# Two expert stages of a hybrid model on one Trainium2 core: a down unit and half a gate unit placed half a slot further back

## The chip, the cores and the metric

The kernel runs on one core of one Trainium2 chip. The metric is the device time in microseconds (us). Every weight comes from device memory (HBM) while the kernel runs, and the same core computes both layers. TensorE, the matmul engine, is called PE in the profile, its weight load PEld; VectorE is DVE, ScalarE is ACT, GpSimd is POOL, and SyncE, which issues nearly all loads, is SP. A DMA instruction issued on SP joins one queue and is served by the core's 16 DMA engines in order of issue. 1 MiB below is 1,048,576 bytes, and a full "unit" of weights is 4 MiB.

## The reference, cut to what matters

Two layers (a recurrent mix, then a gated linear attention) are each followed by a mixture of 32 experts over 272 tokens (256 and 16 meta tokens), all in 32-bit floats. Each token uses 2 experts of one group, but all experts' weights are needed: 3 MiB each, 96 MiB a layer.

```python
def hier_moe(h, w_group, b_group, w_router, b_router, w_gate, w_up, w_down):
    ...
    combine = jnp.sum(jax.nn.one_hot(expert_idx, N_EXPERTS, dtype=jnp.float32) * weights[..., None], axis=1).astype(h.dtype)
    y = jnp.zeros_like(hf)
    for e in range(N_EXPERTS):
        hid = jax.nn.silu(hf @ w_gate[e]) * (hf @ w_up[e])
        y = y + (hid @ w_down[e]) * combine[:, e:e + 1]
    return y.reshape(B, T, D)
```

## The kernel before, in words

An expert stage (`y` = 0 for the first layer, 1 for the second) takes the experts in 8 groups of 4 (`q` = 0 to 7). Tokens are gathered per expert into a tile of at most 32 rows, so that 4 experts fill 128 partitions. Each group has three units of weights: gate, up and down. So a stage has 24 units, `u = 3 * q + kind`, each 4 experts x 2048 floats in each partition (4 MiB). For gate and up the 2048 floats are 8 blocks of 256 over the contraction index k; for down they are 2 blocks of 1024.

There are four slots in the on-chip memory (`slots[0]` to `slots[3]`, each as large as one unit), and `UNIT_SLOT[y][u]` says which slot a unit uses. For units 0 to 11 they simply go round. In the first stage these are slots 1, 2, 3, 0 and again; in the second 0, 1, 2, 3. `UNIT_PREV[y][u]` is the unit that was in the slot before. A slot's lower half of every expert is its columns `0:D` (D = 1024), the upper half `D:2 * D`.

**The load side** is one program on SP, `experts(y)`. It goes through the units in order and issues most units as two DMAs of 2 MiB, each with rows of 8 KiB (line 449). Ahead of each it waits until the unit that was last in the slot is done (line 419, semaphore `unit_done`, which PE raises by one at the end of each unit). A few units at the start of a stage are cut up. Unit 4 (up, q = 1) has its first half laid aside in other buffers (`aside`), and its second half goes to the lower half of its slot as soon as the first half of gate 0 has been used (`half_done`). Unit 5 (down, q = 1) goes half by half: its lower half on `half_done`, its upper half on the unit before it in the slot, unit 1 (lines 421 to 427 for y = 0, lines 444 to 447 for y = 1). In the first stage one expert's quarter of unit 5 (`down[:, 7, 0:D]`) is issued early, at line 406, since a quarter of unit 1 lies elsewhere and leaves that place free. Unit 6 (gate, q = 2) and all that follow wait for a whole slot. After unit 11 SP waits for unit 8, and may load experts for overflowing tokens (lines 452 to 467) into the slot of unit 8; in the first stage of this run that happens once.

**The compute side** is one program on PE. For every group it runs, in this order, the gate unit (line 1531, 64 matmuls), the sums of the group before into the output (`combine`, lines 1491 and 1493), the up unit (line 1531), transposes and gathers (lines 1484, 1590, 1476), and the down unit (line 1603, 32 matmuls of 512 columns). `loaded(u)` makes PE wait for the load. The last down unit of a stage (unit 23) comes in four DMAs of 1 MiB (line 433); two of them (`ld_last0`) must be there for the first call of line 1671. After the first stage the weights of the second layer's projection come in (lines 484 and 488).

Of the kernel before, what the change touches and what calls it, by code (L numbers as in the profile page):

```python
# [14 lines left out]
D = 1024  # L15
KD = D // P
# [15 lines left out]
NU = 3 * NQ  # L32
# [25 lines left out]
UNIT_SLOT = [[1, 2, 3, 0] * 3 + [2, 3, 0, 1, 2, 3, 0, 1, 2, 0, 1, 3], [0, 1, 2, 3] * 3 + [1, 2, 3, 0, 1, 2, 0, 3, 1, 0, 2, 3]]  # L58
UNIT_PREV = [[max([v for v in range(u) if x[v] == x[u]], default=None) for u in range(NU)] for x in UNIT_SLOT]
UNIT_TURN = [[sum(x[v] == x[u] for v in range(u)) for u in range(NU)] for x in UNIT_SLOT]  # L60
FIRST_LAYER = [UNIT_SLOT[0][:NU - 1].count(j) for j in range(4)]
OV_SLOT = [1, 0]
OV_UNIT = 8
OV_NEXT = 15
# [24 lines left out]
def program(nc, a, out, y_dram):  # L89
    ctx = ExitStack()  # L90
    with ctx:
# [61 lines left out]
        def s(name):  # L153
            if name not in S:
                S[name] = sem(name)
            return S[name]
# [135 lines left out]
        def _(sp):  # L292
# [49 lines left out]
            def experts(y):  # L342
# [23 lines left out]
                for u in range(NU):  # L366
# [13 lines left out]
                    if u == 0:  # L380
                        if y == 0:
                            sp.wait_ge(s("oc_set"), NC)
                        else:
                            sp.wait_ge(s("mix_part"), 1)
                    elif u == 1 and y == 1:
                        sp.wait_ge(s("mix_part"), 4)
                    elif u == 3:
                        sp.wait_ge(s("res_done"), (4, 9)[y])
                        sp.dma_start(slots[j][:, 0:2, :], gate[:, 4:6, :]).then_inc(s(f"ld_s{j}"), 16)
                        if y == 0:  # L390
                            sp.wait_ge(s("res_done"), 5)
                            sp.dma_start(slots[j][:, 2, :], gate[:, 6, :]).then_inc(s("ld_wout"), 16)
                            sp.wait_ge(s("res_done"), 6)
                            sp.dma_start(yst[0], up[:, 3, 0:D]).then_inc(s("ld_pv_ys"), 16)
                            sp.dma_start(slots[j][:, 3, :], gate[:, 7, :]).then_inc(s(f"ld_s{j}"), 16)
                            continue
                        sp.wait_ge(s("res_done"), 11)
                    elif u == OV_NEXT:
                        if y == 0:
                            sp.wait_ge(s("ov_free"), passes)  # L400
                        else:
                            sp.wait_ge(s("ov_fin"), y + 1)
                    elif u == 4:
                        set_aside(2 + y)
                        if y == 0:
                            sp.dma_start(slots[UNIT_SLOT[y][5]][:, 3, 0:D], down[:, 7, 0:D]).then_inc(s("ld_lruw_e5"), 16)
                        if y == 0:
                            sp.wait_ge(s("half_done"), 1)
                            sp.dma_start(slots[j][:, 3, 0:D], up[:, 7, 0:D]).then_inc(s("ld_half"), 16)
                            sp.dma_start(slots[j][:, 0:3, 0:D], up[:, 4:7, D:2 * D]).then_inc(s(f"ld_s{j}"), 16)  # L410
                            sp.wait_ge(s("unit_done"), UNIT_PREV[y][u] + 1)
                            sp.dma_start(slots[j][:, 3, D:2 * D], up[:, 7, D:2 * D]).then_inc(s(f"ld_s{j}"), 16)
                            continue
                        else:
                            sp.wait_ge(s("half_done"), 3)
                    elif u == 5 and y == 1:
                        sp.wait_ge(s("half_done"), 4)
                    elif u > 5:
                        sp.wait_ge(s("unit_done"), NU * y + UNIT_PREV[y][u] + 1)
                    src = (gate, up, down)[kind]  # L420
                    if y == 0 and u == 5:
                        sp.wait_ge(s("half_done"), 2)
                        sp.dma_start(slots[j][:, 0:3, 0:D], down[:, 4:7, 0:D]).then_inc(s(f"ld_s{j}"), 16)
                        sp.wait_ge(s("unit_done"), UNIT_PREV[y][u] + 1)
                        sp.dma_start(slots[j][:, 0:3, D:2 * D], down[:, 4:7, D:2 * D]).then_inc(s(f"ld_s{j}"), 16)
                        sp.dma_start(slots[j][:, 3, D:2 * D], down[:, 7, D:2 * D]).then_inc(s("ld_lruw_e5"), 16)
                        continue
                    for h in range(1 if u == 3 else 0, 2):
                        if u == NU - 1:
                            for k in range(2):  # L430
                                c0 = D * k + 512 * h
                                landed = s("ld_lastk") if h == 1 and k == 0 and y == 1 else s(f"ld_last{h}")
                                sp.dma_start(slots[j][:, :, c0:c0 + 512], down[:, 4 * q:4 * q + 4, c0:c0 + 512]).then_inc(landed, 16)  # L433
                        elif u == NU - 2:
                            if h == 0:
                                sp.dma_start(slots[j][:, :, 0:D], up[:, 4 * q:4 * q + 4, 0:D]).then_inc(s("ld_half"), 16)
                            else:
                                for e in (0, 2):
                                    sp.dma_start(slots[j][:, e:e + 2, D:2 * D], up[:, 4 * q + e:4 * q + e + 2, D:2 * D]) \
                                        .then_inc(s(f"ld_s{j}"), 16)  # L440
                        elif u == 4:
                            sp.dma_start(slots[j][:, 2 * h:2 * h + 2, 0:D], src[:, 4 + 2 * h:6 + 2 * h, D:2 * D]) \
                                .then_inc(s(f"ld_s{j}"), 16)
                        elif u == 5:
                            if h == 1:
                                sp.wait_ge(s("unit_done"), NU * y + UNIT_PREV[y][u] + 1)
                            sp.dma_start(slots[j][:, :, D * h:D * h + D], src[:, 4:8, D * h:D * h + D]).then_inc(s(f"ld_s{j}"), 16)
                        else:
                            sp.dma_start(slots[j][:, 2 * h:2 * h + 2, :], src[:, 4 * q + 2 * h:4 * q + 2 * h + 2, :]) \  # L449
                                .then_inc(s(f"ld_s{j}"), 16)  # L450
# [553 lines left out]
        def _(pe):  # L1004
# [452 lines left out]
            def experts(y):  # L1457
# [49 lines left out]
                def loaded(u):  # L1507
                    j = UNIT_SLOT[y][u]
                    pe.wait_ge(s(f"ld_s{j}"), 32 * (FIRST_LAYER[j] * y + UNIT_TURN[y][u] + 1))
                    if y == 0 and u == 1:  # L1510
                        pe.wait_ge(s("ld_pv_ys"), 272)
                    elif y == 0 and u == 3:
                        pe.wait_ge(s("ld_wout"), 80)
                    elif y == 0 and u == 5:
                        pe.wait_ge(s("ld_lruw_e5"), 96)

                def half_gu(u, q, x, ks=range(KD)):
                    if u == 4:
                        pe.wait_ge(s("ld_half"), 64 + 80 * y)
                    for k in ks:  # L1520
                        if x == 0 and k % (4 if q else 2) == 0:
                            pe.wait_ge(s("xg_set"), gathers(y, q, k))
                        for e in range(4):
                            w = gu_w[UNIT_SLOT[y][u]][:, e, k, :]
                            if u == 4 and k < KD // 2 and e < len(aside[y]):
                                w = aside[y][e][:, FF * k:FF * k + FF]
                            elif u == 4 and k >= KD // 2 and (e < 3 or y == 1):
                                w = gu_w[UNIT_SLOT[y][u]][:, e, k - KD // 2, :]
                            elif u == 1 and y == 0 and k < KD // 2 and e == 3:
                                w = yst[0][:, FF * k:FF * k + FF]  # L1530
                            ins = pe.matmul(ps[32 * e:32 * e + 32, 3 * x, 0:FF], xgT[q % 2][:, k, 32 * e:32 * e + 32], w,  # L1531
                                            start=(k == 0), stop=(k == KD - 1))
                        if u < 2 and k == KD // 2 - 1:
                            ins.then_inc(s("half_done"), 1)
# [17 lines left out]
                for q in range(NQ):  # L1552
# [46 lines left out]
                    for hf in range(2):  # L1599
                        for k in range(2):  # L1600
                            for e in range(4):
                                r = slice(32 * e, 32 * e + 32)
                                ins = pe.matmul(ps[r, 4 + hf, :], hidT[:, k, r],  # L1603
                                                dn_w[UNIT_SLOT[y][u]][:, e, k, 512 * hf:512 * hf + 512], start=(k == 0), stop=(k == 1))
                        ins.then_inc(s("dn_done"), 1)
                    gather(ks=range(4, KD)).then_inc(s("g_done"), 1)
                    pe.wait_ge(s("dn_done"), 2 * n + 2)
# [1142 lines left out]
```

## Time and profile before

| what | us |
|---|---|
| median of 3 runs (788.47 to 789.06) | 788.54 |
| time of the profiled execution | 786.11 |
| its span, first to last instruction | 784.2 |
| PE busy in the span | 715.6 |
| share of the DMA queue on which SP issues | 78.5% of 16 engines |

The span is cut into 40 equal slices of 19.6 us; each digit below is a busy share in tenths. The first expert stage computes from about 195 to 413 us (slices 11 to 21, counted from 1), the second from about 571 to 777 us (from slice 30 on).

```profile
PE   8999999999989999899999999999998977786795
PEclk9999999999999998899999999999999998988999
DMA  8654113499999999999999722009999999999995
```

The row DMA shows that the DMA engines are busy almost throughout both stages and in the last part of the work ahead of them. PE is busy there too, and its digits fall only in the second half of the second stage. PEclk is the granted clock.

The chain that ended last, followed back from the last instruction, has these shares by engine:

```profile
PE 55%; DMA 17%; DVE 4%; issue 2%; SPq 2%; PEld 0%; ACT 0%; PEldq 0%; ACTq 0%
```

### The profile page before, as it was taken

Reading aid. Unit: us, or ns where it says so; the run is one execution under the profiler, and the core shown is the slowest. Engines: PE = TensorE matmul, PEld = TensorE weight load, DVE = VectorE, ACT = ScalarE, POOL = GpSimd, SP = SyncE. Lnnn points to the kernel's source line nnn. Section 1 sums busy time; section 2 is a strip of 40 time slices with the busy share of each in tenths; the row PEclk is TensorE's granted clock in tenths of the full one; section 3 lists DMA queues with packets and bytes.
Section 4 is the critical chain, followed back from the end, with each engine's and each line's share of the span. In section 5 each row is a group of like instructions: output and inputs, shape, how many; then the busy total and the mean of one; then the engine's idle time right before and its main releaser. Section 6 shows DMA issues by size and latency. Waiting matters only on the chain.

```text
span 784.2 us, 16721 instructions
## 1 busy us (share of the span) xinstructions
PE 715.6 (91%) x7436; PEld 457.2 (58%) x7436; DVE 324.4 (41%) x688; ACT 205.7 (26%) x414; POOL 32.1 (4%) x99
## 2 busy tenths in 40 slices
PE   8999999999989999899999999999998977786795
PEld 6777787658645564445537746785764533333442
DVE  7476977535353322332246064542445321221222
ACT  2574577215100000000032354530510000000003
POOL 7006000000000000000000000000000000000000
PEclk9999999999999998899999999999999998988999
DMA  8654113499999999999999722009999999999995
GB/s 265 198 104 144 55 56 111 180 422 365 341 424 420 421 419 421 410 421 420 414 353 371 247 85 78 1 16 418 417 386 422 420 421 420 420 421 421 420 407 197
DMA packets 72069, 242.14 MB, mean 309 GB/s; under 512 B 9846, under 2 KB 37612, under 8 KB 51260
## 3 DMA queue, kind: packets, MB, share of 16 engines
q1 hardware_dynamic: 71788, 240.52, 78.5%
q8 instruction: 59, 0.97, 0.5%
q10 hardware_dynamic: 208, 0.54, 0.2%
q14 instruction: 14, 0.11, 0.0%
HBM read 240.00 MB, written 1.05 MB: 307 GB/s over the span
## 4 chain that ended last, share of the span: by engine, by line
PE 55%; DMA 17%; DVE 4%; issue 2%; SPq 2%; PEld 0%; ACT 0%; PEldq 0%; ACTq 0%
PE ps L1531 10%; PE ps L1852 10%; PE ps L1375 7%; DMA M<-in_m_w_gate_dram 6%; DMA M<-in_m_w_down_dram 6%; PE ps L1476 6%; DMA M<-in_m_w_up_dram 4%; PE ps L1491 4%; PE ps L1603 4%; DVE H L2466 1%; PE ps L1390 1%; SPq L433 1%; PE ps L1746 1%; SPq L449 1%; PE ps L1014 1%
## 5 line engine op out<-in xcount | busy, mean ns | idle before, releaser
L1531 PE MATMUL ps<-M 128*32 128x256 f32 x2016 | 124.5, 396 | 18.4 <-DMA M<-in_m_w_gate_dram 10.8
L1531 PEld LDWEIGHTS ps<-M 128*32 128x32 f32 x2016 | 66.5, 114 | 74.7 <-issue 17.5
L1068 PE MATMUL ps<-M 128*128 128x272 f32 x352 | 85.3, 397 | 1.0 <-DVE M L1981 1.0
L1852 PE MATMUL ps<-M 128*128 128x256 f32 (+2 forms) x288 | 79.9, 434 | 0.0
L1476 PEld LDWEIGHTS ps<-M 128*128 128x128 f32 x608 | 71.5, 192 | 12.2 <-issue 11.7
L1476 PE MATMUL ps<-M 128*128 128x128 f32 x608 | 76.9, 278 | 0.0
L1068 PEld LDWEIGHTS ps<-M 128*128 128x128 f32 x352 | 65.6, 190 | 16.3 <-issue 1.7
L1491 PE MATMUL ps<-M 128*128 128x512 f32 (+1 forms) x120 | 62.6, 646 | 7.3 <-DVE H L2466 5.3
L1603 PE MATMUL ps<-M 128*32 128x512 f32 x448 | 55.8, 643 | 13.3 <-DMA M<-in_m_w_down_dram 13.3
L1852 PEld LDWEIGHTS ps<-M 128*128 128x128 f32 x288 | 53.7, 190 | 22.6 <-issue 15.6
L2463 DVE TENSOR_TENSOR H<-H,ps 128x512 f32<-128x512 f32 x60 | 41.2, 687 | 58.6 <-PE ps L1491 58.3
L1375 PE MATMUL ps<-M 128*128 128x512 f32 (+1 forms) x160 | 57.5, 512 | 0.0
L2442 DVE TENSOR_TENSOR M<-ps,gm 128x512 f32<-128x512 f32 x28 | 19.4, 692 | 64.2 <-PE ps L1476 64.2
L1491 PEld LDWEIGHTS ps<-M 128*128 128x128 f32 (+1 forms) x120 | 19.9, 194 | 42.9 <-DVE H L2463 18.1
L812 ACT ACTIVATE M<-ps 128x272 f32<-128x272 f32 x16 | 6.4, 398 | 143.7 <-PE ps L1484 143.7
L1375 PEld LDWEIGHTS ps<-M 128*128 128x128 f32 x160 | 29.6, 190 | 23.0 <-issue 21.5
L810 ACT ACTIVATE M<-ps 128x256 f32<-128x256 f32 x16 | 6.1, 384 | 132.5 <-PE ps L1531 132.5
L1603 PEld LDWEIGHTS ps<-M 128*32 128x32 f32 x448 | 14.9, 117 | 43.5 <-issue 42.3
L2518 DVE COPY M<-ps 128x512 f32<-128x512 f32 x14 | 9.7, 692 | 59.1 <-PE ps L1603 59.1
L2466 DVE TENSOR_TENSOR H<-H,ps 16x256 f32<-16x256 f32 x32 | 13.3, 414 | 31.6 <-PE ps L1493 31.3
L2513 DVE TENSOR_TENSOR M<-M,ps 128x256 f32<-128x256 f32 x16 | 6.7, 420 | 43.5 <-PE ps L1531 43.5
L818 ACT ACTIVATE M<-ps 128x512 f32<-128x512 f32 x16 | 9.6, 597 | 57.6 <-PE ps L1603 54.6
(462 smaller groups left out, 834.3 us busy)
## 6 DMA issues: line engine op xcount, KB each, us to landing
M<-in_m_w_gate_dram SPq DMA_DIRECT2D x31, 2048.0 KB, 18.5
M<-in_m_w_down_dram SPq DMA_DIRECT2D x26, 2048.0 KB, 21.3
M<-in_m_w_up_dram SPq DMA_DIRECT2D x25, 2048.0 KB, 20.7
M<-in_o_w_in_dram SPq DMA_DIRECT2D x12, 1024.0 KB, 9.1
M<-in_e_w_in_dram SPq DMA_DIRECT2D x11, 1024.0 KB, 6.1
M<-in_m_w_down_dram SPq DMA_DIRECT2D x9, 1024.0 KB, 18.6
M<-in_m_w_up_dram SPq DMA_DIRECT2D x8, 1024.0 KB, 17.5
M<-in_e_w_out_dram SPq DMA_DIRECT2D x4, 1024.0 KB, 5.3
```

What stands on the lines that cost most here:

```text
L818: nc.scalar.activation(yst[q % 2][:, 0:512], ps[:, 4, :], ACT.Copy).then_inc(s("ya"), 1)
L1068: ins = pe.matmul(ps[:, n % 4, 0:T], wringE[:, (n // 2) % 4, k, (n % 2) * P:(n % 2) * P + P], (xnE if n else xuE)[:, k], start=(k == 0), s ...
L1375: ins = pe.matmul(res, mixT[:, k, TOK[n]], w_out, start=(k == 0), stop=(k == 7))
L1476: ins = pe.matmul(ps[:, 1 + k // 4, (k % 4) * P:(k % 4) * P + P], xn[:, n, k, :], R[:, n, :], start=(n == 0), stop=(n == nt - 1))
L1491: return pe.matmul(ps[:, bank, :], rt_[:, TOK[n]], ys[:, 512 * hf:512 * hf + 512], start=True, stop=True)
L1531: ins = pe.matmul(ps[32 * e:32 * e + 32, 3 * x, 0:FF], xgT[q % 2][:, k, 32 * e:32 * e + 32], w, start=(k == 0), stop=(k == KD - 1))
L1603: ins = pe.matmul(ps[r, 4 + hf, :], hidT[:, k, r], dn_w[UNIT_SLOT[y][u]][:, e, k, 512 * hf:512 * hf + 512], start=(k == 0), stop=(k == 1))
L1852: ins = pe.matmul(ps[rows, unit % 4, 0:n], lhs(k), rhs(k), start=(k == 0), stop=(k == KD - 1))
L2442: return tt(xgT[q % 2][:, 4 * b:4 * b + 4], ps[:, 1 + b, :].rearrange("p (k t) -> p k t", k=4), gm[:, y, 4 * b:4 * b + 4].unsqueeze(2).to_ ...
L2463: return tt(H[:, n, c], H[:, n, c], ps[:, 6 + j % 2, :], ALU.add)
L2466: ins = tt(H[0:META, 2, c], H[0:META, 2, c], ps[32 * g:32 * g + META, 6 + j % 2, 0:256], ALU.add)
L2518: v.tensor_copy(yst[q % 2][:, 512:1024], ps[:, 5, :]).then_inc(s("yd"), 1)
```

## The change

Both stages get a new placement of units 5 and 6, with `MOVED` = 3 experts in the first stage and 4 in the second. Of unit 5, block k = 0 of the moved experts goes to the upper half of the slot of unit 4 (which held unit 0), and block k = 1 to the lower half of its own slot. Of unit 6, the first half over k of the moved experts goes to the upper half of the slot of unit 5, which unit 5 no longer uses, and the second half to the upper half of its own slot. Every piece has its own wait: unit 5 waits for unit 0, then for the first half of unit 1; unit 6 waits for unit 1, then for unit 2. In the first stage the fourth expert stays where it was. As unit 5 now lies partly in the slot of unit 8, and unit 6 partly in the slot of unit 9, these wait for other units than before: unit 8 for unit 5 (before: unit 4), and unit 9 for unit 6 (before: unit 5). The number of bytes loaded is the same; unit 6 comes in pieces with rows of 4 KiB instead of 8 KiB for its moved experts. The matmuls are the same in number, kind and order; only the address of their weights and two load semaphores differ.

```diff
+MOVED = [3, 4]
+AFTER = {8: 5, 9: 6}
...
-                    elif u == 5 and y == 1:
-                        sp.wait_ge(s("half_done"), 4)
-                    elif u > 5:
-                        sp.wait_ge(s("unit_done"), NU * y + UNIT_PREV[y][u] + 1)
+                    elif u > 6:
+                        sp.wait_ge(s("unit_done"), NU * y + AFTER.get(u, UNIT_PREV[y][u]) + 1)
                     src = (gate, up, down)[kind]
-                    if y == 0 and u == 5:
-                        sp.wait_ge(s("half_done"), 2)
-                        sp.dma_start(slots[j][:, 0:3, 0:D], down[:, 4:7, 0:D]).then_inc(s(f"ld_s{j}"), 16)
-                        sp.wait_ge(s("unit_done"), UNIT_PREV[y][u] + 1)
-                        sp.dma_start(slots[j][:, 0:3, D:2 * D], down[:, 4:7, D:2 * D]).then_inc(s(f"ld_s{j}"), 16)
-                        sp.dma_start(slots[j][:, 3, D:2 * D], down[:, 7, D:2 * D]).then_inc(s("ld_lruw_e5"), 16)
+                    m = MOVED[y]
+                    if u == 5:
+                        sp.wait_ge(s("unit_done"), NU * y + 1)
+                        sp.dma_start(slots[UNIT_SLOT[y][4]][:, 0:m, D:2 * D], down[:, 4:4 + m, 0:D]).then_inc(s("ld_lruw_e5"), 16)
+                        sp.wait_ge(s("half_done"), 2 * y + 2)
+                        if m == 4:
+                            for e in (0, 2):
+                                sp.dma_start(slots[j][:, e:e + 2, 0:D], down[:, 4 + e:6 + e, D:2 * D]).then_inc(s(f"ld_s{j}"), 16)
+                        else:
+                            sp.dma_start(slots[j][:, 0:3, 0:D], down[:, 4:7, D:2 * D]).then_inc(s(f"ld_s{j}"), 16)
+                            sp.wait_ge(s("unit_done"), NU * y + 2)
+                            sp.dma_start(slots[j][:, 3, D:2 * D], down[:, 7, D:2 * D]).then_inc(s(f"ld_s{j}"), 16)
+                        continue
+                    if u == 6:
+                        sp.wait_ge(s("unit_done"), NU * y + 2)
+                        sp.dma_start(slots[UNIT_SLOT[y][5]][:, 0:m, D:2 * D], gate[:, 8:8 + m, 0:D]).then_inc(s("ld_pv_ys"), 16)
+                        sp.wait_ge(s("unit_done"), NU * y + 3)
+                        if m == 4:
+                            for e in (0, 2):
+                                sp.dma_start(slots[j][:, e:e + 2, D:2 * D], gate[:, 8 + e:10 + e, D:2 * D]).then_inc(s(f"ld_s{j}"), 16)
+                        else:
+                            sp.dma_start(slots[j][:, 0:3, D:2 * D], gate[:, 8:11, D:2 * D]).then_inc(s(f"ld_s{j}"), 16)
+                            sp.dma_start(slots[j][:, 3, :], gate[:, 11, :]).then_inc(s(f"ld_s{j}"), 16)
                         continue
...
                             elif u == 4 and k >= KD // 2 and (e < 3 or y == 1):
                                 w = gu_w[UNIT_SLOT[y][u]][:, e, k - KD // 2, :]
+                            elif u == 6 and k < KD // 2 and e < MOVED[y]:
+                                w = gu_w[UNIT_SLOT[y][5]][:, e, k + KD // 2, :]
...
-                                                dn_w[UNIT_SLOT[y][u]][:, e, k, 512 * hf:512 * hf + 512], start=(k == 0), stop=(k == 1))
+                                w = dn_w[UNIT_SLOT[y][u]][:, e, k, 512 * hf:512 * hf + 512]
+                                if u == 5 and e < MOVED[y]:
+                                    w = dn_w[UNIT_SLOT[y][5 - (k == 0)]][:, e, 1 - k, 512 * hf:512 * hf + 512]
+                                ins = pe.matmul(ps[r, 4 + hf, :], hidT[:, k, r], w, start=(k == 0), stop=(k == 1))
```

## Rows read from the trace of the kernel before

**Rows 1.** What the DMA engines moved, GB/s in 40 slices of 19.6 us (page).
```profile
GB/s 265 198 104 144 55 56 111 180 422 365 341 424 420 421 419 421 410 421 420 414 353 371 247 85 78 1 16 418 417 386 422 420 421 420 420 421 421 420 407 197
```
**Rows 2.** Waits of PE, 190 to 450 us: who <- whom: us, times, longest.
```profile
PE ps L1491 <- DVE H L2466: 5.3, 7, 0.8
```
**Rows 3.** The same view, 550 to 784 us.
```profile
PE ps L1603 <- DMA M<-in_m_w_down_dram: 13.3, 4, 3.3
```
**Rows 4.** Issues on SP, first stage, units 7 to 10: start, us, what.
```profile
218.57 1.89 SPq L449 DMA_DIRECT2D M<-in_m_w_up_dram  x2
227.96 0.88 SPq L449 DMA_DIRECT2D M<-in_m_w_down_dram  x2
237.86 0.88 SPq L449 DMA_DIRECT2D M<-in_m_w_gate_dram  x2
243.67 0.88 SPq L449 DMA_DIRECT2D M<-in_m_w_up_dram  x2
```
**Rows 5.** Line 449's issue-to-landing times: unit 11 with its starts, then units 7, 8.
```profile
L449 SPq DMA_DIRECT2D M<-in_m_w_down_dram x2: 368/420/472, 253.1 to 253.5; - x2
DMA to landing us min/median/max: 18.6/20.9/23.2
...
DMA to landing us min/median/max: 13.3/15.4/17.5
...
DMA to landing us min/median/max: 13.9/16.1/18.4
```
**Rows 6.** Two 2 MiB DMAs into an empty queue, issued at 527.3, then 146.9: landing times.
```profile
DMA to landing us min/median/max: 7.9/10.9/13.9
...
DMA to landing us min/median/max: 8.5/10.8/13.1
```
**Rows 7.** One 1 MiB DMA into an empty queue, line 488 at 444.9.
```profile
DMA to landing us min/median/max: 5.2/5.2/5.2
```
**Rows 8.** PE's timeline, units 10, 11, 23: start, us, what, idle before.
```profile
272.83 3.66 PE L1531 MATMUL ps<-M 128*32 128x256 f32 x64
...
280.67 3.64 PE L1603 MATMUL ps<-M 128*32 128x512 f32 x32
...
401.62 1.92 PE L1671 MATMUL ps<-M 128*32 128x512 f32 x16 [0.47 <-ACT M L814]
```
**Rows 9.** Landing times, pairs of units 15 (issued 304.7), 16 (320.4), 17 (329.8).
```profile
DMA to landing us min/median/max: 14.2/16.5/18.7
...
DMA to landing us min/median/max: 8.9/11.5/14.1
...
DMA to landing us min/median/max: 10.0/12.5/14.9
```
**Rows 10.** Line 433, unit 23: landing times; the median is that issued at 382.0.
```profile
DMA to landing us min/median/max: 16.4/18.6/19.5
```
**Rows 11.** Landing times: unit 21 (8 KiB rows, second at 368.0), line 436 (4 KiB, 376.9).
```profile
DMA to landing us min/median/max: 12.4/14.7/17.0
...
DMA to landing us min/median/max: 13.1/13.1/13.1
```
**Rows 12.** Second stage, windows: PE PEld DVE ACT POOL busy, clock, DMA share, GB/s.
```profile
570.00:575.00 5.00, 4.77 (x64) 3.37 (x67) 2.83 (x12) 1.69 (x3) 0.00 (x0) 1.00 0.94 350
575.00:580.00 5.00, 4.77 (x88) 2.78 (x76) 2.50 (x11) 0.38 (x1) 0.00 (x0) 1.00 1.02 404
580.00:585.00 5.00, 4.72 (x42) 3.22 (x46) 1.11 (x2) 0.88 (x3) 0.00 (x0) 1.00 0.99 378
```
**Rows 13.** Issues on SP, second stage, units 8 and 9.
```profile
600.05 0.88 SPq L449 DMA_DIRECT2D M<-in_m_w_down_dram  x2
608.60 0.88 SPq L449 DMA_DIRECT2D M<-in_m_w_gate_dram  x2
```
**Rows 14.** Landing times, second stage, unit 7 (issued 592.3, 592.7).
```profile
DMA to landing us min/median/max: 15.7/17.9/20.2
```
**Rows 15.** PE's timeline: a down unit after a long wait, second stage.
```profile
652.73 5.33 PE L1603 MATMUL ps<-M 128*32 128x512 f32 x32 [3.31 <-DMA M<-in_m_w_down_dram]
```

More of the change, by code:

```diff
@@ L443, in experts @@
                                 .then_inc(s(f"ld_s{j}"), 16)
[L444 to L447, printed above, removed]
                         else:
@@ L1513, in loaded @@
                         pe.wait_ge(s("ld_wout"), 80)
-                    elif y == 0 and u == 5:
-                        pe.wait_ge(s("ld_lruw_e5"), 96)
+                    elif u == 5:
+                        pe.wait_ge(s("ld_lruw_e5"), 96 + 16 * y)
+                    elif u == 6:
+                        pe.wait_ge(s("ld_pv_ys"), 288 + 16 * y)
                 def half_gu(u, q, x, ks=range(KD)):
@@ L1602, in experts @@
                                 r = slice(32 * e, 32 * e + 32)
-                                ins = pe.matmul(ps[r, 4 + hf, :], hidT[:, k, r],
-                                                dn_w[UNIT_SLOT[y][u]][:, e, k, 512 * hf:512 * hf + 512], start=(k == 0), stop=(k == 1))
+                                w = dn_w[UNIT_SLOT[y][u]][:, e, k, 512 * hf:512 * hf + 512]
+                                if u == 5 and e < MOVED[y]:
+                                    w = dn_w[UNIT_SLOT[y][5 - (k == 0)]][:, e, 1 - k, 512 * hf:512 * hf + 512]
+                                ins = pe.matmul(ps[r, 4 + hf, :], hidT[:, k, r], w, start=(k == 0), stop=(k == 1))
                         ins.then_inc(s("dn_done"), 1)
```

## The prediction

> **What bounds the kernel now.** I read the page's slices first, then PE's waits in each stage, then SP's issues with their landing times. The slices show 410 to 424 GB/s through nearly all of both expert stages, with dips to 365 and 341 where the first stage begins, to 386 where the second begins, and to 353 late in the first [rows 1]. So the DMA queue is close to full in both. But that doesn't mean that it bounds both. From 190 to 450 us the list of PE's waits has 14 entries, the largest is on DVE, and none names a DMA [rows 2]: in the first stage every load lands before PE wants it, and what counts is by how much. In the second stage the waits on loads lead the list, with 13.3 us for the down units alone [rows 3]; there the queue is never empty from the first load to the last, and the end comes as soon as the bytes are through. So two questions: does the change move a landing past PE's need in the first stage, and does it give or take idle time of the queue in the second?
>
> **The moved loads, first stage.** The pieces of units 5 and 6 that go out earlier fill some of the dips at the start. PE didn't wait for them, so they are worth nothing there by themselves. The price is at unit 8: it waits for unit 5 instead of unit 4. What SP did at the end of unit 5 was to issue unit 9, at 237.9; at the end of unit 4 it issued unit 8, at 228.0. So unit 8 goes out at 237.9, 9.9 us later, and units 9 and 10 both go out at 243.7, the end of unit 6 [rows 4]. The second DMA of a pair goes out 0.4 after the first, and the largest landing time is its own. SP issues in order, so all later loads stand behind this wait; no other queue carries weights.
>
> Is the queue still full at 237.9? Unit 7's second DMA, issued at 219.4, landed 17.5 us later, at 236.9 [rows 5]. In the changed kernel it lands no later than 237.1: the bytes ahead of it are the same, they are issued no later, and the 4 KiB rows of 3 MiB of unit 6 cost at most 0.2 (below). So the queue runs dry just before unit 8 is issued. Before, unit 8 stood in the queue all the time and landed at 228.4 + 18.4 = 246.8 [rows 5].
>
> **The restart** is the term that decides. The trace has two pairs of 2 MiB into an empty queue. At 527.3 the second landed 14.3 us after the first was issued, at 146.9 it took 13.5 [rows 6]. The pure transfer of a pair in a full queue is 9.9 (unit 11's: 253.5 + 23.2 less 253.1 + 18.6 is 5.0 for one [rows 5]), so a restart adds 3.6 to 4.4. A third row stands beside them: unit 16's pair, issued at 320.4, took 14.5 though something was still in flight [rows 9]. The lowest price that any row has is 2.7 (a single 1 MiB in 5.2 less its 2.5 [rows 7]). I take 14.3, since that pair, like unit 8, has nothing behind it for the next 6 us, while that of 146.9 was followed after 1.3. So unit 8 lands at 237.9 + 14.3 = 252.2, **5.4 us later** than before (4.6 by the 13.5, 3.7 by the lowest price).
>
> The Trainium skill (page "DMA: Bandwidth & Descriptors", Specifications) gives a first-byte latency of about 0.6 us for DMAs issued by SP. By it unit 8 would land near 237.9 + 0.6 + 9.9 = 248.4, an estimate from that page, and only 1.6 late. The 527.3 row disagrees: its first 2 MiB took 7.9, not 5.6.
>
> **Who is late.** From unit 8 on the queue stays full: units 9 and 10 are issued 8.5 us before unit 8 lands, unit 11 at 253.1. So each is 5.4 later than before. Unit 11 landed at 271.7 and 276.7 [rows 5], unit 10's last piece 5.0 ahead of that, at 266.7. Unit 10 comes at 272.1, unit 11 at 282.1. PE begins unit 11's matmuls at 280.7 [rows 8]: a **stall of 1.4 us** that wasn't there. Unit 10 is wanted at 272.8 [rows 8], and passes with 0.7 to spare. Unit 11's cover was 4.0; at the lowest price, 3.7, it just holds.
>
> Next the overflow pass stops PE for 25 us and refills the lead, but not the queue: the queue was full through it, so its delay stays. It shrinks where the queue before had idle time. Units 16 and 17 landed at 320.8 + 14.1 = 334.9 and 330.2 + 14.9 = 345.1 [rows 9]; unit 15's last piece landed at 305.1 + 18.7 = 323.8 [rows 9]. That is 21.3 for 8 MiB that a full queue moves in 19.9, so 1.4 is made good: the queue is then 4.0 late, and stays so, as from there on the slices read 420 [rows 1].
>
> At the end of the stage the cover is thin. The second of unit 23's pieces landed at 382.0 + 18.6 = 400.6 [rows 10], and PE uses it at 401.6 [rows 8]: 1.0 of cover. It lands at 404.6, so PE starts there at 404.6 instead of 401.6, **3.0 us late** (1.4 of it from unit 11). This is the queue's delay less 1.0: 2.2 by the 13.5 price, 1.3 by the lowest. Later loads have more room (the rest of unit 23 lands at 410.3, when PE, itself 3.0 late, wants it at 410.7), and the projection's weights land by 424 to 430 for a stretch that starts at 423 and takes them in turn. Nothing between the stages waits for the clock on the wall: the second stage's first loads are issued when PE and DVE are done with the mix, so the 3.0 passes on whole.
>
> **Second stage.** The same moves, with other numbers. Gain: the queue moved 350, 404 and 378 GB/s in the three windows from 570 to 585, where a full one moves 421 [rows 12]: 0.8, 0.2 and 0.5 us idle. The first belongs to unit 4's issue at 573.1, which the change leaves alone; the others, 0.7, lie where unit 5 now goes out at 576.3 and the first half of unit 6 at 580.1. I take 0.5, between nothing and 0.8 (the whole dip of the slice, 386, is 1.6 [rows 1]). Cost one: unit 6's 4 MiB in 4 KiB rows. A 2 MiB piece of such rows landed 5.1 after the one ahead (376.9 + 13.1 against 368.0 + 17.0 [rows 11]), where one of 8 KiB rows takes 5.0: 0.15 each, 0.3 in all, and 0.2 for 3 MiB. Cost two: unit 8 goes out at 608.6 instead of 600.1 [rows 13]. Unit 7 lands at 592.7 + 20.2 = 612.9 [rows 14], so the queue has 4.3 us left in it, where the first stage had none. That is just what a restart adds (4.4), so 0.1 to 0.2 is lost, at worst 1.1 (unit 16's first stage case, 3.4 in flight, 14.5 in place of 13.4). Unit 8 lands at 623, and PE wants it at 624.8. The sum is -0.5 + 0.3 + 0.2 = **0.0** (-0.8 to +0.9).
>
> **The sum.** First stage +3.0, second 0.0: the profiled execution would go from 786.1 to 789.1, and the median, which lies 2.4 above that execution, from 788.5 to **791.5**. PE's own instructions don't change, so they cost nothing.
>
> **The rivals.**
> *A cheaper restart.* If the queue restarts at 2.7, the first stage loses 1.3, and the total is 789.8 with the second stage at 0.0; with unit 8 landing before about 249.2 (an offset of 2.4 or less to the old time) nothing is lost, since 1.4 is regained and 1.0 covered: 788.5. For it: only the single 1 MiB. Against it: three pairs of this very kind at 13.5 to 14.5. By the skill's latency, above, this rival would be the outcome. Chance 0.16, within 0.2%.
>
> *Faster: the second stage decides.* It is bound by bytes, so idle time saved there is saved in full. If the first stage stays whole, as above, and all of the dip at 568 to 588 (1.6 us [rows 1]) is filled, the time is 786.9. The point from which it decides is unit 8's landing in the first stage at 249.2. Against it: the issue at 573.1 doesn't move, and 4 KiB rows take 0.3 back. Chance 0.07.
>
> *Slower still: the clock.* In the second stage a down unit after a wait of 3.3 us took 5.33 instead of 3.64 [rows 8, 15]. If the new stalls of 1.4 and 1.6 did this, each group would lose up to 1.7. At unit 11 that is hidden by the queue's own delay at the end; at unit 23 it adds up to 1.7: 793.2. Against it: the stalls are half as long. Chance 0.07.
>
> *The change doesn't do what it says*: the early pieces can't fail to go out earlier, as their waits are met at 200.5, 204.5, 576.3 and 580.1; it costs nothing more.
>
> **How the numbers follow.** Forecast, slower by the new stalls at the end of the first stage: 0.70, 790.2 to 792.6. With the clock 0.07 above it, the cheaper restart 0.16 below it, faster 0.07. A measurement of this kernel can tell about 0.2%, 1.6 us, from no change. So slower 0.77, same 0.16, faster 0.07. The range for 8 in 10 takes in the forecast, the clock's case and the upper part of the cheap restart: 789.2 to 793.3.
>
> **What would show it.** After: units 8 to 11 issued at 237.9, 243.7, 243.7, 253.1 and landing 5 us late; a dip near 235 to 242 to some 60% of 421 GB/s; PE's waits of the first stage naming the down loads at lines 1603 and 1671, 3 us in sum; the second stage's start at 530.3 and its length unchanged. Wrong would be: a restart that costs under 2.5, other idle time in the first stage than that at 320 to 345 to make up for it, or a second stage that shortens by over 1.

## The result, and the profile after

The changed kernel is slower. Twelve runs of each on the same chips gave a median of 789.92 us (788.13 to 792.26) against 787.77 us for the kernel before, and the ratio is 1.0040 with a 95% interval of 1.0024 to 1.0056. That is +3.2 us (1.9 to 4.4), where +3.0 was forecast. The median of 789.92 is inside the range of 789.2 to 793.3, though just under the forecast's own stretch of 790.2 to 792.6: the kernel before now has a median of 787.77, 0.8 below the one that the forecast started from. The profiled execution took 789.74 us, with a span of 788.0; that of before took 786.11.

What the DMA engines moved (after, same 40 slices as [rows 1], here 19.7 us each):

```profile
GB/s 268 192 111 135 55 57 109 191 419 357 387 357 387 421 420 421 420 421 420 413 344 371 269 74 88 1 12 415 421 393 414 408 420 421 420 422 420 421 405 188
```

The dip around 200 us is partly filled (387 where 341 stood), but there is a new one right behind it: 357 and 387 where 424 and 420 stood. A finer window shows it whole (columns as in [rows 12]; after, 232 to 242 us; before, this stretch moved 421 GB/s):

```profile
232.00:242.00 10.00, 10.00 (x121) 5.61 (x120) 2.07 (x3) 0.60 (x1) 0.00 (x0) 1.00 0.62 225
```

SP's issues in the first stage, units 7 to 11 (after; compare [rows 4]):

```profile
217.10 0.89 SPq L462 DMA_DIRECT2D M<-in_m_w_up_dram  x2
236.39 0.88 SPq L462 DMA_DIRECT2D M<-in_m_w_down_dram  x2
242.20 0.88 SPq L462 DMA_DIRECT2D M<-in_m_w_gate_dram  x2
243.13 0.99 SPq L462 DMA_DIRECT2D M<-in_m_w_up_dram  x2
251.60 1.05 SPq L462 DMA_DIRECT2D M<-in_m_w_down_dram  x2
```

Between 217 and 236 us SP issues nothing; unit 8 no longer goes out in between. This execution reached the stage 1.5 us sooner than that of before, so all these times lie 1.5 lower than in the forecast. The first matmuls of unit 0, before and then after:

```profile
194.93 1.93 PE L1531 MATMUL ps<-M 128*32 128x256 f32 x32 [0.16 <-DVE M L2447]
...
193.45 1.93 PE L1548 MATMUL ps<-M 128*32 128x256 f32 x32 [0.16 <-DVE M L2466]
```

So the times of one trace can be set against those of the other only when both are counted from here. The landing times of units 7, 8 and 11 (after; compare [rows 5]):

```profile
L462 SPq DMA_DIRECT2D M<-in_m_w_up_dram x2: 372/418/465, 217.1 to 217.5; - x2
DMA to landing us min/median/max: 13.3/15.8/18.3
...
L462 SPq DMA_DIRECT2D M<-in_m_w_down_dram x2: 368/420/472, 236.4 to 236.8; - x2
DMA to landing us min/median/max: 7.6/10.5/13.4
...
L462 SPq DMA_DIRECT2D M<-in_m_w_down_dram x2: 367/504/640, 251.6 to 252.0; - x2
DMA to landing us min/median/max: 23.7/26.0/28.3
```

Unit 7 is through at 217.5 + 18.3 = 235.8, unit 8 goes out at 236.4, and lands at 236.8 + 13.4 = 250.2: 13.8 us for a pair that takes 9.9 in a full queue. Unit 11 lands at 280.3, where it stood at 276.7: 3.6 later by the clock of the trace, 5.1 counted from unit 0. PE's waits that name a load, from 190 to 450 us (after; before there was none, [rows 2]):

```profile
PE ps L1690 <- DMA M<-in_m_w_down_dram: 2.1, 1, 2.1
...
PE ps L1623 <- DMA M<-in_m_w_down_dram: 1.2, 1, 1.2
...
PE ps L1548 <- DMA M<-in_m_w_gate_dram: 1.0, 1, 1.0
```

Lines 1690, 1623 and 1548 are 1671, 1603 and 1531 of before. In PE's timeline they are units 11, 21 and 23 (after; compare [rows 8]):

```profile
280.41 3.64 PE L1623 MATMUL ps<-M 128*32 128x512 f32 x32 [1.22 <-DMA M<-in_m_w_down_dram]
...
388.31 3.66 PE L1548 MATMUL ps<-M 128*32 128x256 f32 x64 [0.99 <-DMA M<-in_m_w_gate_dram]
...
404.41 1.92 PE L1690 MATMUL ps<-M 128*32 128x512 f32 x16 [2.12 <-DMA M<-in_m_w_down_dram]
```

PE starts on unit 23 at 404.4 instead of 401.6, and the first loads of the second stage go out at 530.1 instead of 527.3 (after):

```profile
530.07 0.88 SPq L462 DMA_DIRECT2D M<-in_m_w_gate_dram  x2
```

From unit 0 to this load it took 336.6 us, before 332.4. So the first stage lost **4.3 us**; 1.5 of them don't show in the total of this pair of executions, because the changed one had started its stage sooner. The remaining 1.0 of the total's 3.8 lies behind the load (257.9 us to the end, before 256.9). It can't be put down to the change: six other traces with the second stage of before took 256.5 to 259.2 for it. The same stretch, from unit 0 to the second stage's first load, in every trace (the kernels are those of the next section):

| kernel | from unit 0 to the second stage's first load, us |
|---|---|
| before | 332.4 |
| second stage alone | 334.6 |
| later unit 9 | 332.6 |
| second stage's two waits; its longer wait | 331.6; 331.8 |
| units 8 and 9 by halves | 332.5 |
| 4 KiB rows | 332.8 |
| changed | 336.6 |
| first stage alone, twice | 336.6, 336.5 |
| the waits without the moves, twice | 336.6, 336.4 |
| the longer wait in the first stage | 342.5 |

### The profile page after: what moved, and what is told of

The parts are those of the page before. It is cut to its first block, busy times and chain, and to the rows that moved or that the text cites. A ratio compares the mean times of both kernels' runs of the same rounds, so it can differ in the third digit from the quotient of the medians.

```text
span 788.0 us, 16724 instructions
## 1 busy us (share of the span) xinstructions
PE 718.0 (91%) x7436; PEld 458.1 (58%) x7436; DVE 324.4 (41%) x688; ACT 205.4 (26%) x414; POOL 31.8 (4%) x99
## 4 chain that ended last, share of the span: by engine, by line
PE 50%; DMA 22%; DVE 4%; SPq 3%; issue 2%; ACT 0%; PEld 0%; PEldq 0%; ACTq 0%
DMA M<-in_m_w_down_dram 12%; PE ps L1871 10%; PE ps L1548 9%; PE ps L1388 7%; DMA M<-in_m_w_gate_dram 5%; PE ps L1489 5%; DMA M<-in_m_w_up_dram 4%; PE ps L1623 3%; PE ps L1504 3%; SPq L450 2%; DVE H L2485 1%; PE ps L1403 1%; PE ps L1765 1%; PE ps L1027 1%; PE ps L1423 1%
## 5 line engine op out<-in xcount | busy, mean ns | idle before, releaser
L1548 PE MATMUL ps<-M 128*32 128x256 f32 x2016 | 127.1, 402 | 18.0 <-DMA M<-in_m_w_gate_dram 13.5
L1013 POOL TENSOR_SCALAR M<-M,rs 128x512 f32<-128x512 f32 x1 | 1.6, 1567 | 555.6 <-DVE rs L1987 555.6
## 6 DMA issues: line engine op xcount, KB each, us to landing
M<-in_m_w_up_dram SPq DMA_DIRECT2D x8, 1024.0 KB, 19.7
M<-in_m_w_gate_dram SPq DMA_DIRECT2D x6, 1024.0 KB, 13.7
```

## The experiments

Theory D says that the loss is the queue running dry ahead of unit 8 in the first stage. The rivals put it elsewhere: in the second stage (S), in the moved pieces themselves (M), in PE's clock (C), or in any later wait whatever the queue holds (W). Ratios below are against the kernel before, run on the same chip; 0.001 is 0.8 us.

**The first stage alone.** Everything that the change does, for y = 0 only:

```diff
+CHANGED = (0,)
...
-                    elif u > 6:
-                        sp.wait_ge(s("unit_done"), NU * y + AFTER.get(u, UNIT_PREV[y][u]) + 1)
+                    elif u > (6 if y in CHANGED else 5):
+                        last = AFTER.get(u, UNIT_PREV[y][u]) if y in CHANGED else UNIT_PREV[y][u]
+                        sp.wait_ge(s("unit_done"), NU * y + last + 1)
```

(units 5 and 6 of y = 1 are loaded and read as in the kernel before).

> The change in the first stage alone; the second stage's loads as in the kernel before. Theory D (the queue runs dry ahead of unit 8 of the first stage, which waits for unit 5): the whole of the loss is here, +3.0 us against the kernel before, unit 8 issued some 8.5 to 10 us later, its second DMA landing 13.5 to 14.5 us after the issue, unit 11's matmuls 1.2 to 1.6 late, line of unit 23's first matmuls 3 late in all. Rival S (the loss is in the second stage, where the end hangs on the bytes: 4 KiB rows and the later unit 8 there): +0.0 to +0.5 here. Rival C (TensorE's clock falls after the new stalls): +3 to +5, with matmuls of units 11 and 23 at 5.3 instead of 3.6 us.

Measured: ratio 1.0042 (1.0026 to 1.0059), +3.3 us, so the whole loss is here. Unit 8's pair (first stage alone):

```profile
L477 SPq DMA_DIRECT2D M<-in_m_w_down_dram x2: 368/420/472, 236.1 to 236.5; - x2
DMA to landing us min/median/max: 7.8/10.6/13.3
```

It lands 13.7 after its issue. Rival C expected slow matmuls at units 11 and 23. Unit 11's were not slow, but PE was early at unit 21 and waited 2.9 us there, and then the clock did fall, to 0.69 on average over these 64 matmuls (PE's timeline, first stage alone):

```profile
279.89 3.64 PE L1638 MATMUL ps<-M 128*32 128x512 f32 x32 [0.97 <-DMA M<-in_m_w_down_dram]
388.16 5.29 PE L1563 MATMUL ps<-M 128*32 128x256 f32 x64 [2.90 <-DMA M<-in_m_w_gate_dram]
...
404.10 1.92 PE L1705 MATMUL ps<-M 128*32 128x512 f32 x16 [0.47 <-ACT M L842]
```

The 1.6 us that these 64 matmuls took longer than their usual 3.7 went the way of a shorter wait: unit 23 begins at 404.1, when its load has just come (issued at 385.0, landed 18.7 later, at 403.7), where the changed kernel waited for it and began at 404.4. The same wait of 2.9 to 3.0 at unit 21, with matmuls of 5.1 to 5.4 us behind it, stands in the trace of this kernel's repeat and in both of the waits without the moves; the changed kernel's trace is the only one of the five without it, and all five need 336.4 to 336.6 for the stretch. So here the clock adds nothing to the total, as the queue is as late as PE.

**The second stage alone.** The same kernel with `CHANGED = (1,)`.

> The change in the second stage alone. Theory D: 0.0 (-0.8 to +0.9) against the kernel before; unit 8 is issued with 4 us still in the queue, so that its landing loses 0.1 to 1.1 us. Rival S: +2 to +4. A third reading, that the earlier pieces win idle time here while the first stage loses more than the total: -1.0 to -1.6.

Measured: ratio 1.0013 (0.9995 to 1.0030), +1.0 us (-0.4 to +2.4). Rival S is out, and so is a gain of 1.0 or more that the first stage would hide. This trace shows, though, that the clock can fall at a place where it costs something. Its first stage is that of before, and still (PE's timeline, unit 23, second stage alone):

```profile
401.61 3.30 PE L1705 MATMUL ps<-M 128*32 128x512 f32 x16 [1.97 <-DMA M<-in_m_w_down_dram]
```

After a wait of 2.0 us these 16 matmuls took 3.3 us instead of 1.9, at a mean granted clock of 0.56. In the changed kernel's trace the same matmuls ran at 1.00 after a wait of 2.1. So the length of the wait doesn't decide it alone, and 1.4 of the 334.6 us in the table is this.

**The waits without the moves.** The kernel before, with one edit:

```diff
                     elif u > 5:
-                        sp.wait_ge(s("unit_done"), NU * y + UNIT_PREV[y][u] + 1)
+                        last = {(0, 8): 5, (0, 9): 6}.get((y, u), UNIT_PREV[y][u])
+                        sp.wait_ge(s("unit_done"), NU * y + last + 1)
```

> The kernel before with nothing moved; only the first stage's units 8 and 9 wait for units 5 and 6, as in the changed kernel. Theory D: the waits alone make the loss, +3.0 (2.2 to 3.6): the queue had no more bytes to send without them. Rival M (the moved pieces themselves cost, by their 4 KiB rows or by their collision with the loads around 200 us): 0 to +1 here.

Measured: ratio 1.0068 (1.0045 to 1.0091), +5.3 us (3.5 to 7.2). The two waits alone make the loss, and M in its plain form falls. But it is more than the 3.6 at the upper end of what was expected, and more than the first stage alone, which has the same waits and the moves besides. In the trace the queue does what it did there:

```profile
L450 SPq DMA_DIRECT2D M<-in_m_w_down_dram x2: 368/418/467, 236.1 to 236.5; - x2
DMA to landing us min/median/max: 7.5/10.3/13.2
```

So I ran both once more, side by side.

> The change in the first stage alone, once more, on the same chip and beside the next two. Its ratio was 1.0042 (1.0026 to 1.0059), that of the waits without the moves 1.0068 (1.0045 to 1.0091). If the moved pieces give back nothing of what the waits take (theory D as it stands), the two agree: both +2.5 to +4.5. If the moved pieces give back some 2 us (theory G), this one is 2 us faster than the waits alone again.

> The kernel before with the first stage's two later waits and no moves, once more. Theory D: as e9_stage1_again within 1 us. Theory G: 2 us slower than it.

Measured: 1.0035 (1.0015 to 1.0055) for the first stage alone, 1.0058 (1.0039 to 1.0077) for the waits. By these ratios the kernel with the moves is about 2 us the faster both times, and both times the intervals overlap; by the medians of the runs themselves it is 2.0 us faster the first time and 0.9 the second. The traces show no such gain in the first stage, where the moves are: 336.6 and 336.5 us with them, 336.6 and 336.4 without. In the first pair the profiled executions differ by 2.1 us, and all of it lies in the second stage, whose loads and matmuls are the same in both: 256.9 us from its first load to the end with the moves, 259.2 without. So a gain by the moves is not shown. One loss of about 4 us lies inside the intervals of all five measurements: the changed kernel, the first stage alone twice, and the waits twice.

**More of the same wait.** As the edit above, with `{(0, 8): 6, (0, 9): 6}`: unit 8 waits for unit 6.

> The kernel before, where units 8 and 9 of the first stage both wait for unit 6: unit 8 goes out 5.8 us later than in the changed kernel. Theory D: the queue is dry already, so each further us is lost whole: 5.8 more than the kernel with the wait for unit 5 (e3_wait1), +8.5 to +9.5 against the kernel before. Rival (the loss of that kernel is PE's clock or chance): no such step, +3 to +6.

Measured: ratio 1.0106 (1.0070 to 1.0142), +8.3 us (5.5 to 11.2); theory D had 8.5 to 9.5. The step over the shorter wait is 3.0 or 3.8 us by the two measurements of that, not 5.8, but their intervals leave room for it. In the trace the second stage's first loads go out at 537.9, 8.2 later than with the shorter wait; 2.3 of that this execution had lost before the stage, as its unit 0 begins at 195.4 and not at 193.1. The rest, 5.9, is the step that was expected:

```profile
537.88 0.88 SPq L450 DMA_DIRECT2D M<-in_m_w_gate_dram  x2
```

This execution also shows what a longer stall does to PE (its timeline, unit 9):

```profile
268.03 6.49 PE L1532 MATMUL ps<-M 128*32 128x256 f32 x64 [4.05 <-DMA M<-in_m_w_gate_dram]
```

After 4.1 us of waiting the 64 matmuls took 6.5 instead of 3.7, at a mean granted clock of 0.55. In the changed kernel, whose longest wait in this stage is 2.1, none did.

**A later wait that doesn't empty the queue.** As above, with `{(0, 9): 6}` alone.

> The kernel before, where only unit 9 of the first stage waits for unit 6 instead of unit 5 (5.8 us later); unit 8 goes out as before. Theory D: when unit 9 is issued the queue still holds 3 us of unit 8, so the restart costs only 1.0 to 1.5 at unit 9, of which the idle time of the queue at 320 to 345 makes good the most: 0 to +1.0, a third of the loss of the changed kernel at most. Rival W (any later wait in the prefetch costs its own delay): +3 or more.

Measured: ratio 0.9986 (0.9966 to 1.0005), -1.1 us. Nothing is lost though unit 9 goes out 5.8 us later, so rival W is out. Unit 9's pair (this kernel), issued with 3.1 us of unit 8 still to land, took 14.5, 1.5 more than what was ahead of it and its own 9.9 account for; the idle time later on made it good:

```profile
L450 SPq DMA_DIRECT2D M<-in_m_w_gate_dram x2: 368/420/471, 242.1 to 242.5; - x2
DMA to landing us min/median/max: 9.6/11.8/14.1
```

**The same in the second stage.** First the kernel before with `{(1, 8): 5, (1, 9): 6}`, the second stage's waits of the change:

> The kernel before, where the second stage's units 8 and 9 wait for units 5 and 6; nothing moved. Theory D: 4 us are left in the queue when unit 8 is issued, so the later wait costs 0.1 to 1.1. If the second stage's moves give nothing, this is about what the change in the second stage alone gave (1.0013, 0.9995 to 1.0030).

Measured: ratio 0.9990 (0.9975 to 1.0006), -0.8 us. Unit 8 is issued at 606.4, 4.8 us before unit 7 is through (590.5 + 20.7 = 611.2), and lands at 606.8 + 14.3 = 621.1, which is 9.9 after unit 7:

```profile
L450 SPq DMA_DIRECT2D M<-in_m_w_down_dram x2: 367/418/470, 606.4 to 606.8; - x2
DMA to landing us min/median/max: 9.8/12.0/14.3
```

With 4.8 us left in the queue the restart is hidden whole. Then `{(1, 8): 6}`, which lets it run dry:

> The kernel before, where only unit 8 of the second stage waits for unit 6 instead of unit 4 (614 instead of 600 us). Theory D: the queue runs dry at 612.9, unit 8's second DMA lands 13.5 to 14.5 after its issue, at about 628, and since the second stage ends with the queue, all of the 4.9 to 5.7 shows in the total. A wait for unit 5 instead (the second stage of the changed kernel, 608.6) left 4 us in the queue and cost 0 to 1. Rival (PE's own pace hides it, as PE waits later anyway): 0 to +2.

Measured: ratio 1.0065 (1.0047 to 1.0084), +5.1 us (3.7 to 6.6). Unit 8's pair:

```profile
L450 SPq DMA_DIRECT2D M<-in_m_w_down_dram x2: 368/420/472, 612.4 to 612.8; - x2
DMA to landing us min/median/max: 8.8/11.1/13.4
```

Again 13.8 from issue to landing. One wait more, and from no loss it goes to all of what was expected (4.9 to 5.7): the second stage has no cover, but it has a queue that is 4 to 5 us fuller at this point.

**The changed kernel with units 8 and 9 by halves.**

```diff
                     elif u > 6:
-                        sp.wait_ge(s("unit_done"), NU * y + AFTER.get(u, UNIT_PREV[y][u]) + 1)
+                        sp.wait_ge(s("unit_done"), NU * y + UNIT_PREV[y][u] + 1)
...
+                        elif u in AFTER:
+                            if h == 1:
+                                sp.wait_ge(s("unit_done"), NU * y + AFTER[u] + 1)
+                            sp.dma_start(slots[j][:, :, D * h:D * h + D], src[:, 4 * q:4 * q + 4, D * h:D * h + D]) \
+                                .then_inc(s(f"ld_s{j}"), 16)
```

> The changed kernel, but units 8 and 9 go out by halves in both stages: the lower half as soon as the unit before it in the slot is done (as in the kernel before), the upper half after unit 5 or 6. Theory D: the lower half of unit 8 goes out near 228, so the queue is full at 237.9; unit 8 lands near 246.5 to 247.5 as before, no stall at units 11 and 23, the first stage loses 0.0. The second stage wins 0.0 to 0.5 less 0.3 for 4 KiB rows of unit 6 and 0.3 for those of units 8 and 9: in all -0.3 to +0.5 against the kernel before. If the early pieces are worth something by themselves it shows here: -0.8 to -1.6. Rival M or S: +2 to +3, as the changed kernel.

Measured: ratio 1.0008 (0.9993 to 1.0023), +0.6 us. All moves are still there, and the loss is gone from the first stage too (332.5 us). From 232 to 242 us its queue moved 403 GB/s, where the changed kernel's moved 225, and no load stands among PE's waits of the first stage:

```profile
232.00:242.00 10.00, 9.45 (x94) 6.15 (x98) 2.57 (x6) 0.98 (x2) 0.00 (x0) 1.00 1.01 403
```

It isn't faster than the kernel before either: the early pieces are worth nothing that can be measured.

**The length of the rows.** The kernel before, with units 6 to 9 issued as lower and upper half (4 KiB rows), at the same moments:

```diff
+                        elif u in (6, 7, 8, 9):
+                            sp.dma_start(slots[j][:, :, D * h:D * h + D], src[:, 4 * q:4 * q + 4, D * h:D * h + D]) \
+                                .then_inc(s(f"ld_s{j}"), 16)
                         else:
```

> The kernel before, where units 6 to 9 of both stages are issued as two DMAs of 4 KiB rows (lower half, upper half) in place of two of 8 KiB rows, at the same moments; no wait and no place changes. By the landing times of the trace of before, 0.15 us for each DMA: 8 in each stage, 1.2 us later in the second stage, where it shows in full, and up to 1.2 in the first, where 0 to 1.2 shows: +1.2 to +2.4. If row length costs nothing: 0.0.

Measured: ratio 1.0042 (1.0019 to 1.0065), +3.3 us (1.5 to 5.1), somewhat above the 1.2 to 2.4. In the trace the price of one piece is what was read from before: units 6 and 8, whose DMAs land 5.1 us apart instead of 5.0 (215.2 + 9.6 and 215.6 + 14.3; 230.4 + 14.8 and 230.9 + 19.5):

```profile
DMA to landing us min/median/max: 9.6/11.9/14.3
...
DMA to landing us min/median/max: 14.8/17.2/19.5
```

Sixteen such pieces are 2.4 us. The change has 7 MiB of new 4 KiB rows, not 32: by either figure 0.5 to 0.7 us.

## Why the prediction was right

**What bounds the kernel.** Right. The first stage lives on how early its loads land, the second on the bytes; the two waits cost some 4 us in the first stage (measured in all: 5.3 and 4.6), nothing in the second, and one wait more in the second cost 5.

**The queue runs dry at unit 8.** Right: unit 7 through 0.6 us before unit 8 goes out, and 225 GB/s over ten microseconds.

**The restart.** Forecast 14.3 us for the pair, measured 13.8, and 13.7, 13.6 and 13.8 in three other kernels. It lies between the two rows [rows 6], nearer to the one that I had not taken; I read too much into what stood behind each pair. The lowest price, from a single 1 MiB [rows 7], would give about 12.6, and every pair here took longer. By the first-byte latency of 0.6 us that the Trainium skill gives (page "DMA: Bandwidth & Descriptors", Specifications) it would be 10.5, an estimate from that page. The traces disagree with that too: no such pair here took less than 13.2.

**Who is late.** Unit 11: forecast a stall of 1.4, measured 1.2. Unit 10 passed, as forecast. Unit 21's stall of 1.0 is new. At unit 23 404.6 was forecast and 404.4 measured, but that agreement is luck: this execution had begun 1.5 sooner, so from unit 0 on its unit 23 came 4.3 late, not 3.0. The trace to compare with is the repeat of the first stage alone, which began like that of before (unit 0 at 194.7 against 194.9, the clock at 0.83 in both). There unit 8 landed at 251.3, 4.5 later than before (5.4 was forecast), and unit 17 at 348.6, 3.5 later (4.0). But by unit 21, at 389.6, the queue was 4.6 late again, though both queues moved 419 GB/s on the way; why is open. PE began unit 23 at 405.5, 3.9 late (first stage alone once more: units 0, 8 and 23):

```profile
194.68 1.93 PE L1563 MATMUL ps<-M 128*32 128x256 f32 x32 [0.16 <-DVE M L2481]
...
L477 SPq DMA_DIRECT2D M<-in_m_w_down_dram x2: 368/420/471, 237.6 to 238.0; - x2
DMA to landing us min/median/max: 7.6/10.5/13.3
...
405.51 1.92 PE L1705 MATMUL ps<-M 128*32 128x512 f32 x16 [0.47 <-ACT M L842]
```

**The first stage's sum: the right terms, some of them mis-sized.** Forecast 5.4 for unit 8, less 1.4 made good, less 1.0 of cover, is 3.0. Measured, in that pair of traces: 4.5, of which nothing was made good for long, and PE 3.9 late at unit 23. Against the mean of the five traces in the table that have 8 KiB rows and no loss (332.6), the five with unit 8 behind unit 5 and whole (336.5) took 3.9 longer. So the stage costs about 4 and not 3. That the total came out at +3.2, next to the forecast's +3.0, is in part luck: its interval reaches 4.4.

**The cover at the end of the first stage.** The 1.0 us that the trace of before showed is not a property of the kernel. In four kernels whose first stage is that of before or loses nothing, PE reached the end of the stage sooner and did wait for unit 23. The second stage alone:

```profile
PE ps L1705 <- DMA M<-in_m_w_down_dram: 2.0, 1, 2.0
```

The kernel with the later unit 9 shows 1.9 there, those with the second stage's two waits and its longer wait 1.1 and 1.3. So in many executions the queue sets that end as well, and then its whole lateness counts, not its lateness less 1.0.

**The second stage.** Forecast 0.0 (-0.8 to +0.9), from -0.5 for filled idle time, +0.3 for rows and +0.2 for unit 8. The change alone there gave +1.0 (-0.4 to +2.4), so the term can't be told from its forecast. In the trace of after the gain is hardly there. The windows that stood at 350, 404 and 378 GB/s [rows 12] now read:

```profile
570.00:575.00 5.00, 4.73 (x46) 3.06 (x48) 3.71 (x19) 1.73 (x4) 0.00 (x0) 1.00 1.02 426
575.00:580.00 5.00, 4.75 (x76) 2.88 (x72) 3.25 (x15) 2.07 (x4) 0.00 (x0) 1.00 0.88 333
580.00:585.00 5.00, 4.68 (x69) 3.64 (x62) 0.96 (x3) 0.49 (x2) 0.00 (x0) 1.00 1.02 407
```

Together that is 0.4 us less idle (the windows lie 2.8 earlier in the stage than in the forecast; moved by 2.8 they give 0.4 too). And unit 8 lost more than 0.2: issued at 611.4, 4.3 before unit 7 was through at 595.5 + 20.2 = 615.7, its pair landed at 626.4, 10.7 after it, so 0.8 was lost. In the second stage alone, with the same loads, unit 8 went out at 609.95 with 3.7 left, and landed at 623.7, 10.0 after unit 7: 0.1 lost.

```profile
L462 SPq DMA_DIRECT2D M<-in_m_w_down_dram x2: 368/420/471, 611.4 to 611.8; - x2
DMA to landing us min/median/max: 9.3/11.9/14.6
```

**The rivals.** The cheaper restart: excluded by five pairs between 13.2 and 13.8, the last that of the longer wait. Faster by the second stage: excluded, it gained nothing alone. The clock: not in the profiled execution of the changed kernel, where it stayed at 1.00 after its waits of 1.0, 1.2 and 2.1. In other kernels it fell after waits of 2.0 to 4.1 us; where it fell at unit 21 it took the place of a later wait, but at unit 23, in the second stage alone, it cost 1.4. How often that happens in the changed kernel no trace shows. What stays open is whether the moves give anything back in the total.

## What to carry to other kernels

When a load is placed in space that another, earlier planned load used to claim, cost the load that now has to wait, not the one that moved: what counts is whether the queue still holds something when it is issued. Here a later issue with 3.7 to 4.8 us of transfers left in the queue lost 0 to 0.8, with 3.1 left 1.5, and once the queue was dry it lost the whole restart and, in the traces, every microsecond of further wait. A pair loaded by halves, each on its own wait, kept the queue full with the same placement. A margin read from one execution can be smaller than what the engine's own pace varies by. And before two traces are compared, count both from the same event: by the clock of the trace this loss looks like 2.8 us, from unit 0 on it is 4.3.

## What the runs showed of the hardware that was not expected

- A pair of 2 MiB DMAs took 13.2 to 13.8 us from its first issue to the last landing in each of five kernels in which the queue had run dry, where the same pair behind others adds 9.9. It took 14.5 with 3.1 us left to land, 13.8 with 3.7, 15.0 with 4.3, and 14.7 with 4.8: so a restart is not a fixed price on top of the queue: what is left in it pays for most of it.
- Two executions differ by 1.5 us before any of the changed work starts. From 185 to 195 us the granted clock was 0.83 in the profile of before and 1.00 in that of after, with the same instructions, and 24 matmuls of one gather took 4.54 us in the one (line 1390) and 2.92 in the other. The windows, before and then after:

```profile
185.00:195.00 10.00, 9.05 (x63) 8.21 (x65) 5.94 (x26) 4.66 (x7) 0.00 (x0) 0.83 0.90 353
...
185.00:195.00 10.00, 9.04 (x90) 7.75 (x89) 7.01 (x31) 4.92 (x9) 0.00 (x0) 1.00 0.94 356
```

Of the thirteen profiled executions, four show 0.83 there (before, the halves, the row length, the first stage alone once more) and nine 1.00. What decides it was not looked into. It isn't all that shifts the start: with the longer wait in the first stage unit 0 began at 195.4, with the shorter one at 193.1, at 1.00 in both.
